# Handing out 96 small vector steps anew beside three feed-forward stages

## What is computed

```
def conv_glu_ffn(x, w_up, w_fconv, b_fconv, w_down):        # first model, layers 0 and 1
    a, g = jnp.split(x @ w_up, 2, axis=-1)                  # 1024 -> 2 * 2816
    g = causal_dwconv(g, w_fconv, b_fconv)                  # 3 taps
    return (jax.nn.silu(g) * a) @ w_down                    # 2816 -> 1024

def second_block(x, c, w_ada, b_ada, ...):
    c_act = jax.nn.silu(c)
    for l in range(DEPTH):
        mod = c_act @ w_ada[l] + b_ada[l]                   # 1024 -> 6 * 1024
        sh1, sc1, g1, sh2, sc2, g2 = jnp.split(mod, 6, axis=-1)
        ...                                                 # x + g1 * mix(modulated x)
        h = modulate(rmsnorm(x, norm_ffn_g[l]), sh2, sc2)
        f = swiglu(h, ...) if l == 0 else moe_swiglu(h, ...)
        x = x + g2 * f
```

## Time and profile before

| what | value |
|---|---|
| time, median of 3 runs | 2084.1 us (2083.78 to 2084.38) |
| time of the profiled execution | 2083.09 us |
| its span, first to last instruction | 2081.1 us |
| PE busy with matmuls | 2038.9 us, 98% |
| PE busy loading weights | 1792.9 us, 86% |
| DVE busy | 1754.4 us, 84% |
| ACT busy | 1339.6 us, 64% |
| modulation steps on DVE | 96, mean 1279 ns, 122.8 us busy |
| side loads on SP | 96 of 512 KB, median 4.3 us from issue to landing |
| mean granted TensorE clock | 0.995 of full speed |

### The profile page before, as it was taken

One profiled execution on the slowest core, in us unless ns is written; L12 is line 12 of the kernel. 1 busy time (PEld: TensorE's weight loads), 2 busy tenths in 40 slices (PEclk: granted clock), 3 DMA queues, 4 the chain that ended last, 5 costly groups with the idle time before them and its releaser, 6 DMA issues.

```text
span 2081.1 us, 31128 instructions
## 1 busy us (share of the span) xinstructions
PE 2038.9 (98%) x12718; PEld 1792.9 (86%) x12718; DVE 1754.4 (84%) x2299; ACT 1339.6 (64%) x1839; POOL 3.6 (0%) x23
## 2 busy tenths in 40 slices
PE   9999999999999999999989999999999999999998
PEld 8889999889998789998788888888888888888886
DVE  6779986789987967787869998888989889898987
ACT  4655545655545565445667777777777777777775
POOL 0000000000000000000000000000000000000000
PEclk9999999999999999999999999999999999999999
DMA  5358783348784438785449999999999999999994
GB/s 209 127 196 280 256 299 135 128 185 287 252 302 176 162 112 306 273 301 202 144 165 358 364 362 348 345 363 366 362 351 344 362 365 361 347 351 367 364 359 183
DMA packets 94179, 578.53 MB, mean 278 GB/s; under 512 B 11600, under 2 KB 14672, under 8 KB 35792
## 3 DMA queue, kind: packets, MB, share of 16 engines
q1 hardware_dynamic: 92592, 570.03, 74.0%
q10 hardware_dynamic: 1152, 3.32, 0.4%
q0 software_dynamic: 288, 3.15, 0.4%
HBM read 572.27 MB, written 1.05 MB: 275 GB/s over the span
## 4 chain that ended last, share of the span: by engine, by line
PE 76%; DVE 17%; ACT 5%; DMA 1%; issue 1%; SPq 0%; DVEq 0%; ACTq 0%
PE bank L2061 46%; PE bank L512 28%; DVE wlo L1403 6%; DVE side L1499 2%; DVE arena L1725 2%; DMA ring<-in_w_in 1%; PE bank L2119 1%; ACT arena L1240 1%; DVE RSTD L1471 1%; DVE midl L1715 1%; ACT whi L1027 1%; ACT midh L1229 1%; DVE XC L1480 0%; DVE XC L1460 0%; ACT HH L1082 0%
## 5 line engine op out<-in xcount | busy, mean ns | idle before, releaser
L1027 ACT ACTIVATE whi<-ring 128x1024 fp32r<-128x1024 f32 (+1 forms) x766 | 756.0, 1020 | 148.7 <-PE bank L512 66.1
L1403 DVE TENSOR_TENSOR wlo_moe<-ring,whi 128x1024 fp32r<-128x1024 f32 x448 | 526.4, 1220 | 9.6 <-ACT whi L1027 6.9
L512 PE MATMUL bank<-HH,whi 128*128 128x256 f32 x1536 | 430.6, 280 | 4.3 <-DVE wlo L1403 3.0
L512 PE MATMUL bank<-HL,whi 128*128 128x256 f32 x1536 | 424.3, 276 | 0.0
L512 PE MATMUL bank<-HH,wlo 128*128 128x256 f32 x1536 | 424.3, 276 | 0.0
L1403 DVE TENSOR_TENSOR wlo<-ring,whi 128x1024 fp32r<-128x1024 f32 (+3 forms) x318 | 343.6, 1114 | 76.4 <-ACT whi L1027 76.2
L512 PEld LDWEIGHTS bank<-HH,whi 128*128 128x128 f32 x1536 | 288.4, 188 | 8.7 <-DVE wlo L1403 4.2
L512 PEld LDWEIGHTS bank<-HL,whi 128*128 128x128 f32 x1536 | 288.5, 188 | 0.9 <-issue 0.5
L512 PEld LDWEIGHTS bank<-HH,wlo 128*128 128x128 f32 x1536 | 288.4, 188 | 0.0
L1403 DVE TENSOR_TENSOR extra_lo<-ring,extra_hi 128x1024 fp32r<-128x1024 f32 x224 | 264.4, 1221 | 14.7 <-ACT extra_hi L1027 14.4
L1027 ACT ACTIVATE extra_hi<-ring 128x1024 fp32r<-128x1024 f32 x224 | 229.8, 1061 | 41.1 <-PE bank L2061 41.1
(11 more groups left out here) (293 smaller groups left out, 3463.5 us busy)
## 6 DMA issues: line engine op xcount, KB each, us to landing
ring<-in_moe_gate SPq DMA_DIRECT2D x112, 1024.0 KB, 5.8
ring<-in_moe_up SPq DMA_DIRECT2D x112, 1024.0 KB, 6.7
ring<-in_moe_down SPq DMA_DIRECT2D x112, 1024.0 KB, 5.5
side<-in_w_ada SPq DMA_DIRECT2D x96, 512.0 KB, 4.3
ring<-in_w_up SPq DMA_DIRECT2D x44, 1024.0 KB, 4.9
ring<-in_w_in SPq DMA_DIRECT2D x32, 1024.0 KB, 5.5
ring<-in_w_down SPq DMA_DIRECT2D x32, 704.0 KB, 5.2
ring<-in_ffn_gu SPq DMA_DIRECT2D x22, 1024.0 KB, 4.8
```

The costliest lines, as they stand in the source:

```text
L512: return pe.matmul(out, lhsT, rhs, start=start, stop=stop, skip_group_check=True)
L1027: a.activation(hi, part, ACT.Copy).then_inc(*made.up(("hi", n, i)))
L1403: v.tensor_tensor(lo, part, hi.bitcast(F32), ALU.subtract).then_inc(*done.up(("lo", n, i)))
```

## The change

The thirds are gone. A table, `MOD_AT`, says for each chunk how many modulation steps DVE does in the block of that chunk:

- beside each `w_up`: one in every odd j from 1 to 21, so 11 (before: 21);
- beside each `w_down`: one in both c of m = 0 to 5, and in m = 6 with c = 0, so 13 (before: 11);
- beside `ffn_gu`: two in every odd j, one in every even j from 2 on, so 32 (before: 21);
- beside `ffn_down`: one in both c of all m, so 16 (before: 11).

That is 24, 24 and 48 steps instead of 32, 32 and 32. The steps themselves, their order and their two side buffers stay. SP's generator gives way to a table `mod_loads`: the weights of step n are loaded directly behind the ring load of the chunk that is six places after the chunk of step n - 2, still after a wait for step n - 2. The ring loads, PE's and ACT's programs stay as they were.

```
+        MOD_AT = {}
+        for l in range(DEPTH):
+            MOD_AT |= {("w_up", l, j): 1 for j in range(1, NJ, 2)} | {("w_down", l, m, c): 1 for m in range(7) for c in range(2)}
+            del MOD_AT["w_down", l, 6, 1]
+        MOD_AT |= {("ffn_gu", j): 2 if j % 2 else 1 for j in range(1, NJ)}
+        MOD_AT |= {("ffn_down", m, c): 1 for m in range(8) for c in range(2)}
+        mod_slots = [CH[key] for key in sorted(MOD_AT, key=lambda key: CH[key]) for _ in range(MOD_AT[key])]
...
+        mod_loads = {}
+        for n in range(2, 96):
+            mod_loads.setdefault(mod_slots[n - 2] + 6, []).append(n)
...
+            def mod_beside(*key):
+                for _ in range(MOD_AT.get(key, 0)):
+                    mod_step(next(mod_steps))
...
-                    if j > 0:
-                        mod_step(l, j - 1)
+                    mod_beside("w_up", l, j)
...
-                        mod_step(l, NJ - 1 + 2 * m + c)
+                        mod_beside("w_down", l, m, c)
...
-                    if j > 0:
-                        mod_step(2, j - 1)
+                    mod_beside("ffn_gu", j)
...
-                        mod_step(2, NJ - 1 + 2 * m + c)
+                        mod_beside("ffn_down", m, c)
...
+            def mod_load(n):
+                if n >= 2:
+                    sp.wait_ge(*v_mod("step", n - 2))
+                sp.dma_start(side_in[n % 2], t["w_ada"][n // 48, n // 8 % 6, n % 8]).then_inc(s_side[n % 2], 16)
...
-                for _ in range(steps_behind(chunks[n - NSLOT][0]) if NSLOT <= n < first_moe else 0):
-                    next(mod)
+                for k in mod_loads.get(n, ()):
+                    mod_load(k)
```

More of the change, by code:

```diff
@@ L488, in build @@
         IN = {0: "ln0", 1: ("ln2", 0)}
+        MOD_AT = {}
[5 more added lines that the diff above has]
+        mod_slots = [CH[key] for key in sorted(MOD_AT, key=lambda key: CH[key]) for _ in range(MOD_AT[key])]
+        assert len(mod_slots) == 96, len(mod_slots)
+        mod_loads = {}
+        for n in range(2, 96):
+            mod_loads.setdefault(mod_slots[n - 2] + 6, []).append(n)
         FIRST_ORDER = (4, 5, 6, 7, 0, 1, 2, 3)
@@ L1487, in low_parts, with mod_step @@
                         *v_norm.up((s.name, "hl", k), (s.name, "hl", k + 1)))
[L1489 to L1493, removed]
+            mod_steps = iter(range(96))
+            def mod_step(n):
                 l, i, k = n // 48, n // 8 % 6, n % 8
@@ L2003, in delayed_rows @@
                                      Z[32 * g:32 * g + 32, m, 0:S - r]).then_inc(s_zr[m - 1], 16)
-            mod = modulation()
             for n, (_, src, (a, b), _) in enumerate(chunks):
@@ L2020, in sp_program @@
                 if n == CH["w_out", 0, 3]:
-                    next(mod)
+                    mod_load(0)
+                    mod_load(1)
                 for l in range(DEPTH):
```

## The result

The changed kernel takes 2097.12 us (median of 6 runs, 2092.7 to 2098.47) beside 2083.96 us for the kernel before (6 runs, 2083.11 to 2085.81): ratio 1.0058, 95% interval 1.0045 to 1.0071. It is **13 us slower**; 2075.8 us was forecast. The profiled execution took 2098.06 us, with a span of 2096.1 us, 15.0 us more than that of before.

The account below looks back on a forecast made before the run. PE, 98% busy, was taken to lose time in w_down waiting for late DVE, with low clock behind. Profiled: 2083.09 - 10.8 + 2.5 = 2074.8 us; median 1.0 us higher, 2075.8 us; range 2072.8 to 2079.0 us (85%).

Parts of the forecast that it names:

- Where DVE loses time before the change: Beside w_up DVE falls back 0.18 us a block; PE then waits in w_down, up to 1.61 us, at lower clock.
- Gain of 10.8 us in the convolutional stages: Both w_up/w_down stages: 5.9 + 5.1 = 11.0 us of excess over the gated stage goes, less 2 x 0.1 us stall.
- allowed 0.45 us: In the w_down stages: one pilot matmul of the norm, absent from the gated stage, taken as 0.45 us.
- Rest of w_down: cost nothing: 13 steps instead of 11 beside w_down: cost nothing; if the cover is gone, up to 0.5 us each.
- The stall of 0.5 us at block 21: End of ffn_gu: two steps there make the first m = 1 split ready at 8.0 us against PE's 7.48 us.
- 2.5 us in all behind ffn_down: 16 steps instead of 11: last split at 950.6 instead of 948.11 us, delaying the norm; includes the PE stall.
- Cost nothing, with 0.9 us to spare: Side loads in ffn_gu: asked for 4.7 us before use, landing in 3.8 us, so no cost.
- Rival D: Side loads come late in ffn_gu, landing in 5.8 us: + 17.3 us, so 2093 us; chance 5%.
- Its own price row, 5.8 us: Side-load landing time in ffn_down before the change, where ring and side loads are close together; used to price late loads.
- A's fall of the clock: Rival: PE idle about 2 us at the end of ffn_down, clock falls, costing 1.7 us: 2077.5 us; chance 11%.
- B: Rival: gaps at w_down stay in part, DVE 1 us late, 5.4 us back: 2081.2 us; chance 6%.
- C: Rival: PE is the bound throughout, nothing gained: 2084 us, a little more with ffn_down's 2.5 us; chance 4%.

Follow-up runs that it names:

- half loads: The change with two buffers, side loads from 50 on bringing 512 of 1024 columns while steps still work through 1024: 2082.85 us, ratio 0.9991.

## Why the prediction was wrong

- **Where DVE loses time before the change: right.** The waits at the start of `w_down` and the 1.2 GHz stretch behind them are gone. The kernel before with a third buffer keeps them, so it is the division that took them away.
- **Gain of 10.8 us in the convolutional stages: right as work, 4 us too high as found.** It is 3.96 + 2.71 = 6.7 us in the change, and 5.57 + 4.75 = 10.3 us with three buffers. What is missing in the change are late loads, 5.4 us of DVE's waits in the two stages. The last 0.5 us is the forecast's own: with three buffers both stages take 174.99 us without a wait of PE, 0.8 us more than stage 3 before, where it allowed 0.45 us; "Rest of w_down: cost nothing" held for the DVE work alone.
- **The stall of 0.5 us at block 21, and 2.5 us in all behind ffn_down: right as work.** With three buffers stage 3 is 0.74 us longer than before and its end 1.57 us, 2.3 us together. In the change late loads come on top: the latest of them costs DVE 2.8 us close ahead of the last residual, the end waits 6.52 us, and PE's stall at block 21 is 2.07 us at `midl` with a low clock behind it instead of 0.5 us.
- **SP, "Cost nothing, with 0.9 us to spare": this is the step that failed.** The 4.7 us from asking to use were right. The 3.8 us of landing came from a program in which each load had a block to itself. Where two steps share a block, two loads are asked for some 2 to 3.6 us apart, beside those of the ring, and they land in 5.4 us in `ffn_gu`; in `ffn_down`, where a step stands in every c, it is 6.1 us. And asking to use was worked out for `ffn_gu` alone. Close ahead of the last residual it is no longer either: the load asked for at 950.16 us landed after 7.4 us, and DVE was ready for it after 4.6 us. The prediction even had the price, 1.4 us for 512 KB more at 367 GB/s, but spread it over two blocks instead of laying it on the load that comes behind; 3.8 + 1.4 = 5.2 us would have been an estimate near what was measured, and above 4.7 us.
- **Rival D was the case, at 5%.** Its point of decision, 5.3 us, lay just under the 5.4 us measured. That its 2093 us comes near is in part luck. It laid 17.3 us on `ffn_gu`, where the change lost 7.5 us; by its own sum 5.4 us of landing make (2 x 0.7 - 0.2) x 10 - 2.7 = 9.3 us. And it had nothing for late loads beside `ffn_down`, at its end and beside `w_down`, where the rest was lost. Its own price row, 5.8 us, was the nearest to the new state: `ffn_down` before the change already asked for its loads close together.
- **A's fall of the clock did happen in the change, but behind another wait.** PE waited 6.52 us there and not 2 us, and the twelve matmuls behind it took 4.30 instead of 2.75 us. Little of that reached the time: of the 7.22 us more behind stage 3, 6.36 us are the longer wait and 0.86 us the rest. With three buffers and a wait of 1.73 us the granted clock is 1.00 and the same matmuls take 2.75 us; in its second profile, behind 3.16 us, they take 4.23 us. So at the wait that was forecast it did not happen, at a somewhat longer one it did.
- **B and C were not the case.** In the change PE has no wait at the start of either `w_down`, and the two stages did gain. The Trainium skill (Perfetto Trace Analysis, section Identifying the Most-Contended Engine) says to optimize the engine with the highest occupancy first. Taken as the prediction tried it, with moved DVE work worth nothing, it does not agree with the runs: at the same 98% of PE, 13 us were lost (2097.12 against 2083.96 us) or 9.7 us gained (2074.88 against 2084.57 us), by when DVE gets its data.

What stays open: whether the longer landing is due to the 16 DMA engines (busy 0.92 of the time at 331 GB/s, 0.75 at 264 GB/s with half loads) or to the memory behind them. The runs only show that it comes with asking for more at a time, and that it costs nothing where the asking is early enough.

## What to carry to other kernels

When a change puts two consumers of a double buffer next to each other, compute the time from asking to use afresh, and set against it not the median landing of the old program but the landing in the stretch that is already as crowded as the new one will be. If the difference is under a microsecond or two, count the loads as late, above all ahead of a step that others wait for. One more buffer, asked for one step earlier, was worth 17 to 21 us in the change, 8 us where steps only stood close together, and nothing in the kernel that did not need it.

## What the runs showed of the hardware

- Landing time of a 512 KB load in `ffn_gu`: 3.7 us with one a block (283 GB/s in the window), 5.3 to 5.7 us with three in two blocks and no stalls (331 GB/s in the first of these runs); the ring's 1 MB loads beside them went from 4.8 us to between 6.7 and 7.2 us.
- The same kernel (the change with three buffers) was profiled twice, with its first three-product matmul at 144.97 and at 143.41 us. The window from 20 to 24 us in the two:

```profile
20.00:24.00 4.00, 4.00 (x12) 3.21 (x12) 3.42 (x6) 3.71 (x8) 0.00 (x0) 0.59 0.23 96
```
```profile
20.00:24.00 4.00, 4.00 (x20) 3.54 (x19) 3.42 (x6) 3.71 (x8) 0.00 (x0) 1.00 0.21 88
```

The granted clock was low near the start in one (0.59 of full speed in the mean of these 4 us, between the levels of 1.2 and 2.4 GHz) and not in the other, with the same program, and the first stage began 1.56 us later. The changed kernel's profile has 0.73 in this window. So the + 1.54 us at its start can't be put down to the change.
